# Two-block layer on one core: token scaling, first weights, context squares and the output weights' remainders reordered

## The reference, cut to what matters

```python
sh1, sc1, ... = split(silu(c) @ w_ada + b_ada, 6)       # also for c_ctx
hx = rms_norm(x, norm_mix) * (1 + sc1) + sh1
q, zf_f, zf_b, i, g, gate_b, gate_c, v = split(hx @ w_in)
# context (256 tokens): the same norm and modulation, gates, two start states
# gated linear attention both ways, a short convolution, w_out, router, 16 experts
```

```python
q, kv, gates, c = split(rmsnorm(h) @ w_in_2)
o = three-branch attention(q, kv, gates)      # compressed, selected, window
y_a = o @ w_o_nsa
c = causal_dwconv(c_val * sigmoid(c_gate), conv_w, conv_b)   # 31 taps, 512 channels
h = h + (ga * y_a + gb * (silu(layernorm(c)) @ w_conv_out)) @ w_out   # then a feed-forward
```

## Time and profile before

| | us |
|---|---|
| median of the runs shown (2210.47 to 2213.38) | 2212.53 |
| profiled execution, whole | 2208.05 |
| its span | 2206.3 |
| TensorE products busy | 2048.1 (93%) |
| VectorE busy | 897.4 (41%) |
| ScalarE busy | 569.7 (26%) |
| chain of waits | PE 84%, DMA 6%, DVE 5%, issue 3%, ACT 2% |

### The profile page before, as it was taken

The page is one execution under the profiler, slowest core; times in us unless marked ns, Lnnn a source line. Parts: engine busy times, 40 slices in busy tenths (PEclk is TensorE's granted clock), DMA queues, the critical chain, the costliest instruction groups (busy, mean ns, idle before and its releaser), DMA issues.

```text
span 2206.3 us, 23733 instructions
## 1 busy us (share of the span) xinstructions
PE 2048.1 (93%) x9948; PEld 1269.8 (58%) x9948; DVE 897.4 (41%) x1443; ACT 569.7 (26%) x879; POOL 61.9 (3%) x107
## 2 busy tenths in 40 slices
PE   6999999899998988989899888997999999999998
PEld 4888777443423333333434234764687788888877
DVE  3666674320101111111111002777976456666453
ACT  4534313100000000000000003347435343334453
POOL 1000000000000000000000000014200000000000
PEclk8999999899999999999999999999999999999999
DMA  8552116699999999999999993141122323231220
GB/s 294 193 204 101 39 42 264 250 388 419 428 427 427 428 428 428 427 427 427 428 428 428 427 427 154 64 110 39 62 92 77 124 77 101 90 113 69 105 96 39
DMA packets 107178, 529.06 MB, mean 240 GB/s; under 512 B 14925, under 2 KB 43713, under 8 KB 82241
## 3 DMA queue, kind: packets, MB, share of 16 engines
q1 hardware_dynamic: 107073, 527.55, 59.9%
HBM read 525.43 MB, written 2.10 MB: 239 GB/s over the span
## 4 chain that ended last, share of the span: by engine, by line
PE 84%; DMA 6%; DVE 5%; issue 3%; ACT 2%; ACTq 0%; SPq 0%; DVEq 0%
PE bank L988 21%; PE bank L595 14%; PE bank L596 14%; PE bank L597 14%; PE bank L1039 6%; DMA f<-in_w_gate_dram 5%; PE bank L949 3%; PE bank L962 3%; PE bank L606 2%; DVE f L2354 1%; PE bank L848 1%; PE bank L1129 1%; ACT high L1705 1%; PE bank L794 1%; DVE high L2302 0%
## 5 line engine op out<-in xcount | busy, mean ns | idle before, releaser
L988 PE MATMUL bank<-f,high 128*64 128x512 f32 x2048 | 470.7, 605 | 47.0 <-issue 30.2
L595 PE MATMUL bank<-r 128*128 128x512 f32 (+1 forms) x1016 | 404.0, 398 | 12.6 <-DVE high L2125 4.7
L596 PE MATMUL bank<-r 128*128 128x512 f32 (+1 forms) x1016 | 398.8, 392 | 0.0
L597 PE MATMUL bank<-r 128*128 128x512 f32 (+1 forms) x1016 | 398.4, 392 | 0.0
L988 PEld LDWEIGHTS bank<-f,high 128*64 128x64 f32 x2048 | 152.1, 138 | 335.3 <-issue 320.3
L2277 DVE SCALAR_TENSOR_TENSOR f<-bank,low,f 128x512 f32<-128x512 f32 x64 | 48.0, 751 | 510.7 <-PE bank L962 510.7
L1039 PE MATMUL bank<-f,high 128*64 128x512 f32 x1024 | 232.2, 611 | 20.8 <-issue 20.8
L595 PEld LDWEIGHTS bank<-r 128*128 128x128 f32 (+1 forms) x1016 | 191.2, 188 | 68.2 <-issue 16.4
L1415 ACT ACTIVATE high<-bank 128x512 f32<-128x512 f32 (+2 forms) x93 | 51.3, 583 | 679.8 <-PE bank L606 336.2
L596 PEld LDWEIGHTS bank<-r 128*128 128x128 f32 (+1 forms) x1016 | 191.2, 188 | 42.4 <-issue 1.7
L597 PEld LDWEIGHTS bank<-r 128*128 128x128 f32 (+1 forms) x1016 | 190.8, 188 | 41.6
(11 more groups left out here) (353 smaller groups left out, 1781.8 us busy)
## 6 DMA issues: line engine op xcount, KB each, us to landing
f<-in_w_down_dram SPq DMA_DIRECT2D x66, 2048.0 KB, 21.9
f<-in_w_up_dram SPq DMA_DIRECT2D x64, 2048.0 KB, 21.7
f<-in_w_gate_dram SPq DMA_DIRECT2D x63, 2048.0 KB, 21.5
f<-in_w_in_dram SPq DMA_DIRECT2D x14, 2048.0 KB, 7.8
f<-in_w_up_dram SPq DMA_DIRECT2D x22, 1024.0 KB, 7.1
high<-in_w_ada_dram SPq DMA_DIRECT2D x32, 512.0 KB, 5.3
f<-in_w_ada_dram SPq DMA_DIRECT2D x4, 2048.0 KB, 17.4
f<-in_w_out_dram SPq DMA_DIRECT2D x4, 2048.0 KB, 7.9
```

The lines of the kernel that those rows point to most:

```text
L595: pe.matmul(o, wh, xh, start=first, stop=False)
L596: pe.matmul(o, wl, xh, start=False, stop=False)
L597: return pe.matmul(o, wh, xl, start=False, stop=last)
L988: ins = pe.matmul(o[64 * e:64 * e + 64, :], xsT[p % 2][:, 2 * k + r, 64 * e:64 * e + 64], ws[e](2048 * r + 512 * fc), start=k == 0 and r = ...
```

## The change

In the front, the program makes the following steps. A root with no use is taken before the squares, and the wait for all constants becomes one for the small constant. ZF comes in four transfers with a semaphore each. On VectorE the copy of PT stands before the reciprocal, and all four tiles are scaled before the first copy of a turned tile. On TensorE tiles 0 and 1 are turned, then come `ada_columns(2)`, tile 2, `ada_turned(2)`, `ada_columns(0)`, tile 3, `ada_turned(0)`. ZF's piece 0 is divided on both engines before tile 3's copies. The context's squares and root come after ZF's piece 3 on ScalarE, and the context's reciprocal and scaling after the last `token_rest` on VectorE. In the attention stage WO2 is divided one piece per unit (ScalarE units 2 to 5, VectorE units 4 to 7), and fewer taps stand in units 4 to 7; the rest is taken up by the call at L2541, which does what is left of the 124.

```diff
--- before.py
+++ after.py
@@ -17,7 +17,7 @@
-DMA_SEMS = (*(f"g{i}" for i in range(6)), *(f"cg{i}" for i in range(4)), "x0", "x1", "rows0", "rows", "small", "ctx", "ada0", "ada1", "ada2", "ada3", "w0", "w1", "ptok", "out",
+DMA_SEMS = (*(f"g{i}" for i in range(6)), *(f"cg{i}" for i in range(4)), *(f"zf{i}" for i in range(4)), "x0", "x1", "rows0", "rows", "small", "ctx", "ada0", "ada1", "ada2", "ada3", "w0", "w1", "ptok", "out",
             *(f"m{i}" for i in range(7)), "mx", "my", "mh0", "mh1")
@@ -323,7 +323,8 @@
         KD = [(0, 8), (8, 8), (16, 6)]
-        chunks = [(cols(win, c0, 512), 4096, True) for c0 in (512, 1536, 1024, 0, 2048, 3072)]
+        chunks = [(quartered(cols(win, 512, 512)), 4096, True)]
+        chunks += [(cols(win, c0, 512), 4096, True) for c0 in (1536, 1024, 0, 2048, 3072)]
         chunks += [(cols(win, c0, 512), 4096, True) for c0 in (3584, 2560)]
@@ -350,7 +351,7 @@
         for c in range(NC_):
-            n_dma[pair[c]] += 0 if c == CG else 16 * len(chunks[c][0](own(SLOT, slot_at[2 * pair[c]])))
+            n_dma[pair[c]] += 0 if c in (ZF, CG) else 16 * len(chunks[c][0](own(SLOT, slot_at[2 * pair[c]])))
             landed.append(n_dma[pair[c]])
@@ -370,8 +371,8 @@
             for i in pieces:
-                if c == CG:
-                    a.wait_ge(s[f"cg{i}"], 16)
+                if c in (ZF, CG):
+                    a.wait_ge(s[f"{'zf' if c == ZF else 'cg'}{i}"], 16)
                 elif i == 0:
@@ -410,7 +411,7 @@
                 for i, (dst, src) in enumerate(chunks[c][0](whole(c))):
-                    sp.dma_start(dst, src).then_inc(s[f"cg{i}" if c == CG else f"w{pair[c]}"], 16)
+                    sp.dma_start(dst, src).then_inc(s[{ZF: f"zf{i}", CG: f"cg{i}"}.get(c, f"w{pair[c]}")], 16)
@@ -650,15 +651,21 @@
-            for t in range(4):
-                if t > 1:
-                    ada_columns(ada_order[t - 2])
-                    ada_turned(ada_order[t - 2])
+            def tokens_turned(t):
                 pe.wait_ge(s["v_pre"], val("v_pre", "xn", t))
...
                        "pe_pre", "xt", t, half)
+
+            tokens_turned(0)
+            tokens_turned(1)
+            ada_columns(ada_order[0])
+            tokens_turned(2)
+            ada_turned(ada_order[0])
+            ada_columns(ada_order[1])
+            tokens_turned(3)
+            ada_turned(ada_order[1])
@@ -1441,11 +1448,12 @@
+            a.wait_ge(s["consts"], val("consts", "eps"))
+            a.activation(small[:, 592:593], epst, ACT.Sqrt)
             for i in range(4):
...
                 up(a.activation(xn[:, i, :], xtok[:, i, :], ACT.Square, accum_out=ss[:, i:i + 1]), "a_pre", "sqx", i)
-            a.wait_ge(s["consts"], val("consts", "all"))
             a.wait_ge(s["a_pre"], val("a_pre", "sqx", 3))
@@ -1453,6 +1461,8 @@
             for t in range(4):
+                if t == 3:
+                    a_divide(a, ZF, [0])
                 if t > 1:
@@ -1463,11 +1473,12 @@
-            a_divide(a, ZF, [0])
-            rounded_tokens((0, 1))
             a_divide(a, ZF, [1])
-            rounded_tokens((2, 3))
+            rounded_tokens((0, 1, 2, 3))
             a_divide(a, ZF, [2])
+            ada_tmp(3)
+            ada_tmp(1)
+            a_divide(a, ZF, [3])
             a.wait_ge(s["ctx"], 16)
@@ -1476,9 +1487,6 @@
             up(a.activation(ss[:, 4:6], ss[:, 4:6], ACT.Sqrt, bias=epst, scale=1.0 / D), "a_pre", "rc")
-            ada_tmp(3)
-            ada_tmp(1)
-            a_divide(a, ZF, [3])
             rounded_tokens((4, 5, 6, 7))
@@ -1748,8 +1756,8 @@
                     exps(un + 2, 1)
-                if un in (2, 3):
-                    a_divide(a, WO2, [2 * un - 4, 2 * un - 3])
+                if un in (2, 3, 4, 5):
+                    a_divide(a, WO2, [un - 2])
                 if un in (3, 4, 6):
@@ -1906,10 +1914,13 @@
             up(v.memset(flat(CP), 0.0), "cp0")
+            v.wait_ge(s["pe_pre"], val("pe_pre", "pt"))
+            up(v.tensor_copy(PT[:, 0, :], bank("pt")[:, 0:128]), "v_pre", "pt")
             v.wait_ge(s["a_pre"], val("a_pre", "rs"))
             up(v.reciprocal(ss[:, 0:4], ss[:, 0:4]), "v_pre", "rs")
-            v.wait_ge(s["pe_pre"], val("pe_pre", "pt"))
-            up(v.tensor_copy(PT[:, 0, :], bank("pt")[:, 0:128]), "v_pre", "pt")
+            v.wait_ge(s["v_pre"], val("v_pre", "rs"))
+            for t in range(4):
+                up(v.tensor_scalar(xn[:, t, :], xtok[:, t, :], ss[:, t:t + 1], None, ALU.mult), "v_pre", "xn", t)
@@ -1919,12 +1930,12 @@
             for t in range(4):
-                if t > 1:
-                    ada_bias(ada_order[t - 2])
-                v.wait_ge(s["v_pre"], val("v_pre", "rs"))
-                up(v.tensor_scalar(xn[:, t, :], xtok[:, t, :], ss[:, t:t + 1], None, ALU.mult), "v_pre", "xn", t)
+                if t == 3:
+                    ada_bias(ada_order[0])
+                    v_divide(v, ZF, [0])
                 v.wait_ge(s["pe_pre"], val("pe_pre", "xt", t, 1))
                 up(v.tensor_copy(XT[:, 4:8, 128 * t:128 * t + 128], v3(bank("xt", t, 1)[:, :], 4)), "v_pre", "xt", t, 1)
+            ada_bias(ada_order[1])
@@ -1947,7 +1958,6 @@
             modulated(1)
-            v_divide(v, ZF, [0])
             token_rest(0)
@@ -1956,11 +1966,6 @@
             v_divide(v, ZF, [2])
-            v.wait_ge(s["a_pre"], val("a_pre", "rc"))
-            up(v.reciprocal(ss[:, 4:6], ss[:, 4:6]), "v_pre", "rc")
-            own_wait("v_pre")
-            for t in range(2):
-                up(v.tensor_scalar(ctok[:, t, :], ctok[:, t, :], ss[:, 4 + t:5 + t], None, ALU.mult), "v_pre", "cn", t)
             ada_bias(3)
@@ -1973,6 +1978,11 @@
             token_rest(7)
+            v.wait_ge(s["a_pre"], val("a_pre", "rc"))
+            up(v.reciprocal(ss[:, 4:6], ss[:, 4:6]), "v_pre", "rc")
+            own_wait("v_pre")
+            for t in range(2):
+                up(v.tensor_scalar(ctok[:, t, :], ctok[:, t, :], ss[:, 4 + t:5 + t], None, ALU.mult), "v_pre", "cn", t)
             a0, a1 = col["lb"][:, 0:8], col["lb"][:, 8:16]
@@ -2516,10 +2526,10 @@
                     low_output(un // 2 - 1)
-                if un in (3, 4):
-                    v_divide(v, WO2, [0, 1] if un == 3 else [2, 3])
+                if un > 3:
+                    v_divide(v, WO2, [un - 4])
                 if un > 1:
-                    conv_taps(2 if un < 5 else 5)
+                    conv_taps(2 if un < 4 else 1 if un < 5 else 3)
             low_output(3)
...
```

## The result

The kernel before took 2212.94 us (median of 4 runs, 2210.47 to 2213.38), the changed one 2193.52 us (median of 4 runs, 2193.17 to 2197.43): ratio 0.9919, 95% interval 0.9901 to 0.9936. That is 19.4 us less, against a forecast of 2194.6. The changed kernel was run again in a later batch: 2195.63 us (6 runs, 2191.96 to 2197.40) against 2210.83, ratio 0.9930 (0.9918 to 0.9942), 15.2 us less. The ten runs together have a median of 2194.3. The profiled execution took 2193.52 us for a span of 2191.8, 14.5 less than the profiled execution of before. The 0.1% of agreement between runs that stands at the start is too narrow: over all runs of this case the kernel before took 2205.83 to 2213.79 us, and the changed one 2191.96 to 2197.43.

What follows compares the result with a forecast made beforehand. It took the expert stage as bound by its weight stream, and two short stretches, front and attention, as TensorE waiting. Gains of 9.6 + 8.3 = 17.9 us gave 2190.2 profiled, plus 4.5 a median of 2194.6; range 2189.5 to 2203.

Steps and rivals of the forecast that it cites:

- (a): Start of the front: a dummy root ahead of the squares saves a 1.29 us table load; first turn at 12.17.
- (b): Front: all tokens scaled first, tiles 0 and 1 turned without a gap; first columns from 15.7, second from 20.5.
- (c): Front: first weights in four transfers, first quarter landing at 21.9; projection starts at 27.2 and not at 37.18.
- half-clock rival: Front: the clock stays at 1.2 GHz until the projection; front gain 7.6, total 15.9, 2196.6 us; chance 0.15.
- (d): First projection: the last w_ada chunk's landing at 36.8 caps the gain; columns end at 38.6, front gain 9.6 us.
- (e): Front: the context's squares, table load and root, 3.9 us, just fit after piece 3; cost 0 to 0.6 us.
- (f): Attention, unit 3: two remainders, 2.35 us, go to units 4 to 7; TensorE's 3.91 us wait falls to 1.6.
- (g): Attention, behind TensorE's 3.91 us wait: the clock stays at 2.4 GHz, making 8 us of work 3.7 us shorter.
- rival with 0.17 of chance: Attention: the clock falls anyway, or ScalarE or GpSimd become the bound; gain 4.6, total 14.2, 2198.3 us; chance 0.17.
- (h): Attention, from unit 4's low part: VectorE's chain goes from 24.7 to 22.4 us; attention gain 8.3, without the clock 4.6.
- (i): End of the taps: the seven taps put off, 5.3 us, fit into VectorE's idle of 7.47 us.
- slower rival: Expert stage: the queue runs dry for 3 us in each of eight expert pairs, costing 24; 2218.6 us; chance 0.04.

Runs made afterwards that it cites:

- e_no_first_root: The changed kernel without the useless root ahead of the squares, so the table loads between squares and root: 2195.99 us (ratio 0.9936 to the kernel before).
- e_ctx_early: The changed kernel with the context's squares, root and scalings back in their old places: 2200.51 us (ratio 0.9955 to the kernel before).
- before_again: The kernel before, unchanged, run again for a second trace: 2209.01 us (ratio 0.9990).
- e_one_transfer: The changed kernel with the first weights in one transfer in place of four: 2198.97 us (ratio 0.9940 to the kernel before).
- e_unit3_taps: The changed kernel with unit 3's last two taps moved into unit 4's idle on VectorE: 2188.86 us (ratio 0.9906 to the kernel before).

## Why the prediction was right, and where it was not

The direction, the range and the forecast held: 2193.52 against 2194.6. By its steps:

- (a), the root's table: no load stands between squares and root, the root ends at 11.13 (11.06 predicted), and the first turn came at 12.18 (12.17 predicted). But the step counted this as front gain, and e_no_first_root shows it is worth 0.0: the same plan had the second columns wait for a landing at 20.5, and I did not draw the conclusion. In the kernel before the table load starts 0.08 us behind the squares and lasts 1.28 us, with the root right behind it. The Trainium skill's page ScalarE: Activation LUTs, section What ACT_TABLE_LOAD costs, gives the load itself 1283 ns, which the trace bears out, and the whole switch 2.66 us, which it does not.
- (b) and (c), the order and the quarters: first columns 15.65 (15.7), second 20.51 (20.5), first piece rounded from 21.79 (landing at 21.9), first modulated tile 25.09 (25.2), projection 27.17 (27.2). The three further issues cost nothing, as assumed: the context's transfer was issued at 22.27, against 22.30. The first columns ran at the full rate, 1.92 us, right behind turns alone, so the half-clock rival did not come about. The Trainium skill's page TensorE: Matmul & The Clock Gate, section Part 4: PE-mode transpose, which gives that case, is not borne out here. In the eleven profiles with the new order the same columns took 1.92 to 3.02 us, 3.02 in e_ctx_early, and in none the 3.64 of columns that are slow throughout; the second ones took 1.92 or 1.93 in all. That is chance, and covered by the landing.
- (d), the cap: the columns end at 38.98 (38.6), front gain 9.34 (9.6), but not by the landing. The step took the old 7.5 us for two steps; behind 2.71 us of idle the first twelve products were slow, and work, not the transfer, set the end. In e_no_first_root the last columns came behind 0.90 us of idle, as they do in seven of the eleven profiles of the new order, five times at 36.70 to 37.11 and twice at 38.03 and 38.04: there the landing did, and the gain was the same 9.35. The two limits lie 0.3 us apart, as the step said.
- (e), the context: fits with 0.3 us to spare. What it prevents, 4.4 to 5.4 us, was never priced.
- (f), the wait: 1.24 (1.6).
- (g), the clock, is the step that failed. It argued that idle of 3.91 us lets the clock fall and that the rest would not. The idle that was left, 1.24 and 0.73 us, was enough in 5 of 7 profiles, the changed kernel's two among them. So the stage gave 6.17 us and not 8.3. This was the rival with 0.17 of chance, which gave an attention gain of 4.6.
- (h), VectorE's chain: from the end of unit 4's low part at 1538.2 to TensorE's restart at 1560.0 it is 21.8 us (22.4); it was 24.8. That makes 3.0 of the 6.17. The other 3.1 are the wait (3.91 - 1.24 = 2.67) and a slightly shorter slow stretch. Where the clock held at first, the gain was 8.3 and 8.6: the figure predicted for that case, although with a later fall of 1.6 in it that the step did not know.
- (i), the tail: 7.47 less 2.12 is 5.35 (5.3), hidden.

The sum was 17.9; the trace shows 9.34 + 6.17 = 15.5, less 0.9 in stages that were not touched. The forecast came out nearer than its parts, and that is luck: it set the gain against the profiled execution and then added 4.5 us because that execution was below the median. Measured by medians the gain is 19.4 in one batch and 15.2 in the other, 17.3 in the mean. Part of the remainder is the yardstick: against before_again, 2.3 us later at the end of the attention stage, the changed kernel's first profile is 16.9 ahead there and not 14.6. For the rest I can show only its form. Several traces lose or gain about 1.6 us at places that no edit touches. TensorE's timeline of the changed kernel shows one such place:

```profile
294.74 0.50 PE L596 MATMUL bank<-r 128*128 128x512 f32 x1 [1.21 <-DVE high L2135]
...
295.73 0.63 PE L596 MATMUL bank<-r 128*128 128x512 f32 x1
```

Eight products last 0.61 to 0.63 us and follow each other at 0.43 where others do at 0.23; the clock reads 0.67 in the 5 us from 295.4, and the lead over the kernel before goes from 9.64 to 8.07. The first profile of before has the same wait of 1.21 us at its same place, 304.38, and no slow product behind it; before_again has them, as shown above. Over all 14 profiles the clock fell at this place in 12. So this step is a clock that fell in one execution and held in the other, behind the same wait of the same code. Whether the steps inside the expert stage are the same thing was not tried.

The slower rival, an expert queue run dry, had no sign: 427 GB/s and a DMA share of 1.01 from 700 to 900, as in the earlier trace rows.

## What to carry to other kernels

Before an edit is priced, follow its gain to the next thing that is late: an edit in front of a wait for a transfer is worth nothing (the dummy root), and an innocent wait for the next phase's data would have cost 4.4 to 5.4 us once the phase before it got faster (the context's squares). On an engine that sits between two others, put work that nobody waits for into its own idle, ahead of the wait, and only as much as fits. A wait of TensorE just over a microsecond cost its own length here and then, in some profiles, as much again or more in slow products (1.6 us behind one of 1.21, 3.3 behind one of 1.24); removing it entirely was worth more than shortening it.

## What was not expected of the hardware

TensorE's clock fell to 1.2 GHz behind 1.24 and 0.73 us of idle, with 0.55 us of turns between them, in 5 of 7 profiles, and made the products behind it 3.3 us longer each time; it fell behind one wait of 1.48 or 1.49 us in e_one_transfer and e_no_first_root, and not behind the same wait in e_unit3_taps. At one and the same place it fell in before_again and held in before, behind the same 1.21 us. Much of what parts the traces of one kernel is made of such steps: they part by 1.3 to 1.6 us at once and run in parallel between. That the spread of the runs without a profile has the same source is not shown. A single profile of two kernels therefore can't tell an edit worth under 3 us. The difference over one stage does better if the clock and the landings are read with it: to 0.3 us in the attention stage, and only to about 1 us in the front.
